# Moving a low-part subtraction from GpSimd to VectorE, and the attention output tiles out of PSUM by ScalarE

## What is computed

```python
def attend(q, k, v, lam):
    s = einsum('bhmqd,bhmkd->bhmqk', q, k) * (B_QK ** -0.5)
    p = softmax(s)
    w = p[:, :, 0] - lam * p[:, :, 1]
    return einsum('bhqk,bhkv->bhqv', w, v)

def diffattn_out(o, subln_w, lam_init):
    return (rmsnorm(o, subln_w) * (1.0 - lam_init)) ...
y_b = diffattn_out(attend(...)) * silu(bz)
```

## Time and profile before

| | |
|---|---|
| median of 3 runs | 2773.3 us (2772.2 to 2774.69) |
| profiled execution | 2774.32 us, span 2772.5 us |
| mean granted TensorE clock | 0.932 |
| PE busy | 2469.1 us (89%) |
| DVE busy | 1277.5 us (46%) |
| ACT busy | 1020.1 us (37%) |
| POOL busy | 882.3 us (32%) |
| POOL low parts, L2552, 254 instructions | 567.2 us |
| DVE low parts, L1833, 254 instructions | 377.3 us |

### The profile page before, as it was taken

The page is one execution under the profiler, slowest core; times in us unless marked ns, Lnnn a source line. Parts: engine busy times, 40 slices in busy tenths (PEclk is TensorE's granted clock), DMA queues, the critical chain, the costliest instruction groups (busy, mean ns, idle before and its releaser), DMA issues.

```text
span 2772.5 us, 39336 instructions
## 1 busy us (share of the span) xinstructions
PE 2469.1 (89%) x16496; PEld 2207.5 (80%) x16496; DVE 1277.5 (46%) x2428; ACT 1020.1 (37%) x1845; POOL 882.3 (32%) x594
## 2 busy tenths in 40 slices
PE   6999999988868999959889998987888999988998
PEld 3877768877756897848879888987767999857998
DVE  4322222555642212453333664236655674556673
ACT  2333312333331222234333444344244444344443
POOL 2222322422211233223335443442312454312453
PEclk9899999999989999978989999998899999989999
DMA  5211124211112312222214223444212455303444
GB/s 229 87 61 61 46 92 167 77 46 61 46 61 94 140 71 76 85 64 92 92 63 150 92 77 117 152 159 142 102 47 106 156 181 177 125 31 107 154 176 142
DMA packets 50416, 291.51 MB, mean 105 GB/s; under 512 B 8960, under 2 KB 13312, under 8 KB 19072
## 3 DMA queue, kind: packets, MB, share of 16 engines
q1 hardware_dynamic: 50240, 289.00, 29.4%
HBM read 286.89 MB, written 2.36 MB: 104 GB/s over the span
## 4 chain that ended last, share of the span: by engine, by line
PE 73%; DVE 14%; ACT 5%; DMA 3%; issue 2%; POOL 2%; SPq 1%; DVEq 0%; ACTq 0%; POOLq 0%
PE PS L478 71%; DMA raw<-in_wpk 2%; ACT wh L1304 2%; DVE TM L1814 2%; DVE wl L1833 2%; PE PS L482 2%; DVE colS L1822 1%; ACT TM L1294 1%; DVE HYl L1822 1%; DVE TM L1822 1%; POOL wl L2552 1%; ACT TMG L1294 1%; POOL TM L2544 1%; DVE small L1814 1%; ACT HYh L1294 1%
## 5 line engine op out<-in xcount | busy, mean ns | idle before, releaser
L2552 POOL TENSOR_TENSOR wl<-raw,wh 128x768 fp32r<-128x768 f32 (+2 forms) x254 | 567.2, 2233 | 1437.9 <-ACT wh L1305 1437.7
L478 PE MATMUL PS<-HYh,wh 128*128 128x256 f32 (+1 forms) x3000 | 966.7, 322 | 63.6 <-DVE HYl L1822 30.6
L478 PE MATMUL PS<-HYl,wh 128*128 128x256 f32 (+1 forms) x3000 | 948.8, 316 | 0.0
L478 PE MATMUL PS<-HYh,wl 128*128 128x256 f32 (+1 forms) x3000 | 946.9, 316 | 0.0
L1833 DVE TENSOR_TENSOR wl<-raw,wh 128x1280 fp32r<-128x1280 f32 (+2 forms) x254 | 377.3, 1485 | 748.7 <-ACT wh L1304 748.6
L478 PEld LDWEIGHTS PS<-HYh,wh 128*128 128x128 f32 x3000 | 589.9, 197 | 114.3 <-DVE HYl L1822 35.6
L478 PEld LDWEIGHTS PS<-HYh,wl 128*128 128x128 f32 x3000 | 588.2, 196 | 31.8
L478 PEld LDWEIGHTS PS<-HYl,wh 128*128 128x128 f32 x3000 | 589.5, 197 | 29.5
L1294 ACT ACTIVATE TM<-PS 128x512 f32<-128x512 f32 (+5 forms) x315 | 163.3, 530 | 772.6 <-PE PS L478 600.7
L1304 ACT ACTIVATE wh<-raw 128x1280 fp32r<-128x1280 f32 (+2 forms) x254 | 306.4, 1206 | 374.3 <-PE PS L478 219.1
L478 PE MATMUL PS<-wh,HYh 128*128 128x256 f32 x1458 | 429.3, 294 | 10.1 <-DVE HYl L1822 5.4
(11 more groups left out here) (174 smaller groups left out, 2041.6 us busy)
## 6 DMA issues: line engine op xcount, KB each, us to landing
raw<-in_wpk SPq DMA_DIRECT2D x235, 1024.0 KB, 4.8
raw<-in_wpk SPq DMA_DIRECT2D x32, 704.0 KB, 4.1
TM<-in_wpk SPq DMA_DIRECT2D x4, 1024.0 KB, 18.2
X<-in_xin SPq DMA_DIRECT2D x1, 2048.0 KB, 10.0
Y<-in_wpk SPq DMA_DIRECT2D x2, 1024.0 KB, 23.9
Y<-bias_d SPq DMA_DIRECT2D x4, 512.0 KB, 9.7
raw<-in_wpk SPq DMA_DIRECT2D x3, 512.0 KB, 3.8
T<-in_tabs SPq DMA_DIRECT2D x1, 1216.0 KB, 14.7
```

Source lines behind the costliest of these rows:

```text
L478: return P.x.matmul(o, l, r, start=start, stop=stop)
L2552: G.x.tensor_tensor(wl[:, s, c:n], raw[:, r, c:n], wh[:, s, c:n], ALU.subtract).then_inc(*lo_rest.mark(u))
```

## The change

It has two parts.

The low part of columns c:n is made by DVE too, as a second instruction right behind the first; POOL's `convert` and all its calls are taken out, with the signal `lo_rest`. PE and SP wait for `lo_split` alone.

In branch B, ACT writes the squares of a tile into `b_yt` and then copies bank 5's part over them, and the event `b_osq` stands for this copy. There are two `b_yt` now, used by turns, and two sets of four sums. PE's wait for `b_yo` before a new group is gone; ACT waits instead, at the first tile of a group, until PE has turned the `b_yt` of two groups before. DVE's root and four products, now from and to `b_yt` in SBUF, stand at `b_done_slot`, in layer 0 one slot later than before; the output step of layer 0 stands eight and four slots behind the last value product, where it was three.

```diff
@@ b_yt, slots
-        b_yt = tm(9728, [4, 128])
-        b_p, b_junk = TMG[:, 0:1024].rearrange("p (m k) -> p m k", m=2), TMG[:, 1024:1152]
+        b_yt = [x.rearrange("p (i c) -> p i c", i=4) for x in (tm(9728, [512]), TMG[:, 1024:1536])]
+        b_p = TMG[:, 0:1024].rearrange("p (m k) -> p m k", m=2)
+        def b_done_slot(l, p, g):
+            if l == 0 and p == 3:
+                return (71, 73)[g]
+            return b_value_slot(l, p, 4 * g + 3) + (2, 1)[l]
         def b_out_slot(l, p, g):
             if p == 3:
                 return (72, 74)[g] if l == 0 else 58
-            return b_value_slot(l, p, 4 * g + 3) + (3, 3)[l]
+            return b_value_slot(l, p, 4 * g + 3) + ((8, 4), (3,))[l][g]
@@ TensorE
             def weights(u):
                 P.wait_ge(lo_split, u)
-                P.wait_ge(lo_rest, u)
...
                     if before := b_prev(l, *pj):
                         P.wait_ge(act_step, ("b_osq", l, *before))
-                        if pj[1] % 4 == 0:
-                            P.wait_ge(dve_step, ("b_yo", l, before[0], before[1] // 4))
@@ ScalarE
                     A.wait_ge(pe_step, ("b_pv", l, *pj))
-                    if i == 0 and (before := b_prev(l, *pj)):
-                        A.wait_ge(dve_step, ("b_yo", l, before[0], before[1] // 4))
+                    k = b_group(l, pj[0], pj[1] // 4)
+                    if i == 0 and k >= 2:
+                        A.wait_ge(pe_step, ("b_yt", l, *((pj[0] - 1, pj[1] // 4) if l == 0 else (pj[0] - 2, 0))))
+                    y = b_yt[k % 2][:, i]
+                    act(y, bank(5)[:, 128 * i:128 * i + 128], ACT.Square, scale=128.0 ** -0.5, accum_out=colC[:, 44 + 4 * (k % 2) + i:45 + 4 * (k % 2) + i])
                     A.wait_own(act_step)
-                    act(b_junk, bank(5)[:, 128 * i:128 * i + 128], ACT.Square, ("b_osq", l, *pj), scale=128.0 ** -0.5,
-                        accum_out=colC[:, 32 + i:33 + i])
+                    act(y, bank(5)[:, 128 * i:128 * i + 128], ACT.Copy, ("b_osq", l, *pj))
@@ VectorE, convert
-                c, s, r = cut_of(u), slot(u), u % NRAW
+                n, c, s, r = words[u], cut_of(u), slot(u), u % NRAW
                 D.wait_ge(hi_split, (u, 0))
-                D.x.tensor_tensor(wl[:, s, 0:c], raw[:, r, 0:c], wh[:, s, 0:c], ALU.subtract).then_inc(*lo_split.mark(u))
+                D.x.tensor_tensor(wl[:, s, 0:c], raw[:, r, 0:c], wh[:, s, 0:c], ALU.subtract).then_inc(*lo_split.mark())
+                D.wait_ge(hi_split, (u, 1))
+                D.x.tensor_tensor(wl[:, s, c:n], raw[:, r, c:n], wh[:, s, c:n], ALU.subtract).then_inc(*lo_split.mark(u))
@@ VectorE, slot_b
-                if (pj := B_VALUES[l].get(n - 1)) and pj[1] % 4 == 3:
-                    p, g = pj[0], pj[1] // 4
-                    k = b_group(l, p, g)
-                    D.wait_ge(act_step, ("b_osq", l, *pj))
-                    root(small[:, 40:44], small[:, 44:48], colC[:, 32:36], more=colC[:, 36 + 4 * (k % 2):40 + 4 * (k % 2)])
+                if pg := B_DONE[l].get(n):
+                    p, g = pg
+                    k = b_group(l, p, g) % 2
+                    D.wait_ge(act_step, ("b_osq", l, p, 4 * g + 3))
+                    root(small[:, 40:44], small[:, 44:48], colC[:, 44 + 4 * k:48 + 4 * k], more=colC[:, 36 + 4 * k:40 + 4 * k])
                     D.wait_own(dve_step)
-                    if k:
-                        D.wait_ge(pe_step, ("b_yt", l, p - (g == 0), 0 if l or g else 1))
                     for i in range(4):
                         a, t_, nk = b_tile(l, 4 * g + i)
-                        stt(b_yt[:, i], bank(5)[:, 128 * i:128 * i + 128], small[:, 40 + i:41 + i], b_z[p % 2][:, t_, a], ALU.mult, ALU.mult,
-                            ("b_yo", l, p, g))
+                        stt(b_yt[k][:, i], b_yt[k][:, i], small[:, 40 + i:41 + i], b_z[p % 2][:, t_, a], ALU.mult, ALU.mult, ("b_yo", l, p, g))
@@ GpSimd: gone, with all its calls
-            def convert(u):
-                if u is None:
-                    return
-                n, c, s, r = words[u], cut_of(u), slot(u), u % NRAW
-                G.wait_ge(hi_split, (u, 1))
-                G.x.tensor_tensor(wl[:, s, c:n], raw[:, r, c:n], wh[:, s, c:n], ALU.subtract).then_inc(*lo_rest.mark(u))
@@ SyncE, load
                     if units[b][1] == "conv":
                         S.wait_ge(lo_split, b)
-                        S.wait_ge(lo_rest, b)
```

More of the change, by code:

```diff
@@ L245, in program @@
         dve_step = signal("dve_step")
-        lo_rest = signal("lo_rest")
         pool_step = signal("pool_step")
@@ L415, in program @@
                                        for f in (b_score_slot, b_turn_slot, b_value_slot))
-        B_OUT = [{b_out_slot(l, p, g): (p, g) for p in range(4) for g in range(2 - l)} for l in range(2)]
+        B_DONE, B_OUT = ([{f(l, p, g): (p, g) for p in range(4) for g in range(2 - l)} for l in range(2)] for f in (b_done_slot, b_out_slot))
         B_QK = ({13: 0, 15: 1}, {10: 0, 11: 1})
@@ L774, in slot_b @@
                     for i in range(4):
-                        t = turned(bank(6)[:, 128 * i:128 * i + 128], b_yt[:, i])
+                        t = turned(bank(6)[:, 128 * i:128 * i + 128], b_yt[b_group(l, *pg) % 2][:, i])
                     t.then_inc(*pe_step.mark(("b_yt", l, *pg)))
@@ L2544, in tt @@
                 return G.x.tensor_tensor(o, a, b, op).then_inc(*pool_step.mark(*events))
-            def convert(u):
-                if u is None:
-                    return
-                n, c, s, r = words[u], cut_of(u), slot(u), u % NRAW
-                G.wait_ge(hi_split, (u, 1))
-                G.x.tensor_tensor(wl[:, s, c:n], raw[:, r, c:n], wh[:, s, c:n], ALU.subtract).then_inc(*lo_rest.mark(u))
-            def used(tag, j):
-                convert(unit_after(place[tag, j]))
             def branch_a(l):
                 t0, N = lay(l)
-                used("gate", l)
                 G.wait_ge(dve_step, ("a_rc", l))
@@ L2570, in branch_a @@
                         tt(a_g[:, c, 0:N], a_g[:, c, 0:N], a_hs[:, c, 0:N], ALU.mult, ("a_gate", l, h))
-                    used("a_z", 4 * l + h)
                     for j in range(4):
@@ L2601, in merge @@
                             total(7)
-                    used("m_" + br, 8 * l + j)
             def merge_b(l):
                 t0, N = lay(l)
-                for j in range(4):
-                    used("m_b", 8 * l + j)
                 for j in range(8):
@@ L2610, in merge_b @@
                     tt(Y[:, j, t0:512], Y[:, j, t0:512], B_GATES[j][:, 0:N], ALU.add, ("m_sum", l, "b", j))
-                    if j % 2:
-                        used("m_b", 8 * l + 4 + j // 2)
             def branch_b(l):
@@ L2700, in second_block @@
                         rope(f"ab_q{2 + j}", tm(3584 + 512 * j, [2, 256]), 2, rope1d, 128)
[L2701 to L2705, removed]
-                else:
-                    for tag, j in (("cq", 0), ("ckv", 0), ("d_q", 0), ("d_q", 1), ("d_k", 0), ("d_k", 1), ("d_v", 0), ("d_v", 1)):
-                        used(tag, j)
+                else:
                     for i in range(3):
                         rope(f"qc{i}", QC[:, 2 * i:2 * i + 2], 2, ropec, 96)
-                    used("uq", 0)
                     rope("qc3", QC[:, 6:8], 2, ropec, 96)
-                    used("ukv", 0)
                     G.wait_ge(dve_step, "kr_rope")
-                    G.wait_own(lo_rest)
                     G.wait_own(pool_step)
@@ L2719, in second_block @@
                     G.wait_own(pool_step)
-                    for j in range(4):
-                        used("cd_out", j)
-                for j in range(2):
-                    used("x_q", 2 * l + j)
-                for j in range(2):
-                    used("x_o", 2 * l + j)
                 def mid(j):
@@ L2731, in second_block @@
                 for j in range(22):
-                    used("gu", 22 * l + j)
                     if j:
@@ L2735, in second_block @@
                 mid(21)
-                for j in range(8):
-                    for i in range(2):
-                        used("dn", 16 * l + 2 * j + i)
             for o, v in ((o1024, 1 / 1024), (o128, 1 / 128), (o256, 1 / 256), (one, 1.0)):
@@ L2742, in pool_program @@
             G.x.memset(sc[:], 0.0).then_inc(*pool_step.mark("sc_zero"))
-            convert(converted[0])
             for l in range(2):
@@ L2747, in pool_program @@
                     tt(H[1][:, k], xs[:, k], H[0][:, k], ALU.subtract, ("H", l, k))
-                    if l == 0 and k == 3:
-                        convert(converted[1])
                 if l == 0:
@@ L2758, in pool_program @@
                 merge(l, "c")
-                for j in range(4):
-                    used("w_out", 4 * l + j)
             for l in range(2):
@@ L2820, in program @@
         programs = (tensor_program, scalar_program, vector_program, pool_program, sync_program)
```

(2 more changed lines are left out.)

16 lines of the change are left out of this document (removed).

## The result

| | before | changed |
|---|---|---|
| median | 2773.31 us | 2704.42 us (2695.15 to 2704.77, 4 runs) |
| ratio | | 0.9743, 95% interval 0.9722 to 0.9765 |
| profiled span | 2772.5 us | 2702.7 us |
| mean granted clock | 0.932 | 0.941 |

What follows compares the result with a forecast made beforehand. PE, busy 89%, was taken as the bound, with its waits mainly for DVE's results, held up partly by POOL. Terms -46.6 - 1.8 - 16.5 + 12.0 = -52.9 us gave 2720.5 us, range 2700 to 2752.

Steps and rivals of the forecast that it cites:

- the lock: DVE instructions with two SBUF inputs and POOL instructions reading SBUF exclude each other; one pair showed 1.85 against 0.42 us.
- the 8.2 us: Layer 0, three PE stalls at a new group's first value product, waiting for `b_yo` while POOL's work slows DVE's root.
- Part 1: Output tiles: removing waits for `b_yo` was to gain 46.6 us in layer 0 and 1.8 us in layer 1.
- the five long stalls: Layer 0 waits on `b_yo`: three of 8.2 us, and two beside the merge of 7.58 and 7.06 us.
- The new wait: Layer 0, after each 8.2 us stall: PE would wait 1.6 us for the next tile's softmax shares.
- Part 2: Low parts moved from POOL to DVE: 16.5 us gained from locks, 12 us lost at steps that only pay.
- my places: Among 122 PE gaps, 29 locked places gaining 16.5 us after paying 0.86 each, and 12 steps that only pay.
- rival 3: The locks are worth more than found on PE's path: another 25 us goes, 2696 us; chance 0.11.
- The wait that is handed on: Layer 0: the next tile's softmax replaces `b_yo`, root still locked by POOL's rotary step; 2749 us, chance 0.18.
- Slower: DVE's second low part falls ahead of steps PE waits for; with 110 of 254, 2803 us; chance 0.08.
- The wait at 167.99: PE's wait of 2.75 us for two products behind a DVE low part, to grow to 3.6 us.
- the signs: Profile after: no group-start wait over 3 us between 555 and 830, POOL near 315 us, DVE about 1390, clock above 0.932.

Runs made afterwards that it cites:

- low parts alone: Against the kernel before, only the second low part moved from POOL to DVE, branch B as before: 2748.45 us, ratio 0.9907.
- Output tiles alone: Against the kernel before, only ACT's copy of output tiles and the later slots, POOL still making its low parts: 2715.41 us, ratio 0.9787.
- the run with the early root: Changed kernel with DVE's root and products of layer 0 one slot earlier, output step at its late slots: 2712.96 us, ratio 0.979.
- the two runs that change its length: Changed kernel with DVE's second low part made twice: 2804.31 us; with it cut to 128 of 768 columns from the fifth unit on: 2651.9 us.
- the run with both engines: Output tiles as changed, POOL making its low parts as before, DVE also running a second subtraction of the same width: 2868.45 us, ratio 1.0349.
- the old slots: Changed kernel with layer 0's root, products and output step at their former slots: 2719.67 us; with only root and products one slot earlier: 2712.96 us.

## Why the prediction came out as it did

**What bounds the kernel, the lock and the reason of the 8.2 us: right.** PE is held up by the root through bank 5, and the root in part by POOL: 3.5 of its 5.9 us are lock. The rest of the 8.2 us is DVE's order, a low part and a reduce ahead of the root, and low parts alone left 7.39 us. Output tiles alone, 2715 us, is what this reading gave for part 1 (-46.6 - 1.8 = 48 us) and more.

**Part 1, size: 46.6 forecast in layer 0, 57.3 measured alone, and 59.6 with part 2.** The term that was too small is the clock. I had 8.5 us behind the five long stalls, from windows of 2.7 to 8 us behind each, and 38.1 us of standing still. With the output tiles alone PE's busy time in the stretch fell by 253.59 - 236.86 = 16.7 us and its standing still by 40.6; the mean clock of the whole stretch went from 0.88 to 0.97. So 8.2 of the 10.7 us missed are clock, twice what I had counted. The new wait that I put at 1.6 us for each of the three long stalls is about 0.75 in the changed kernel: I had the softmax of the next tile late, and overlooked what the new `b_done_slot` does. It puts the root behind the shares. That step was passed over as "one slot later", and the 10 to 13.5 us of the run with the early root hang on it. On the other side, the forecast put no charge on bank 6 beyond a few tenths; the changed kernel waits there twice, 1.8 us each.

**Part 2, forecast net -4.5 us (-16.5 and +12), measured -11 to -14 as the difference to the output tiles alone** (in stages +14 and -29). The sum came out near, its terms did not. The second piece costs 0.33 to 0.40 us on the path for each of its microseconds, by the two runs that change its length. 248 us of it are then 82 to 99 us, where my places gave 12 + 25 = 37. As the sum is -11 to -14, POOL's low parts must have cost some 95 to 110 us, where I had 41 (16.5 and the 25 paid at those places). This last number is an estimate from a slope on both sides of the changed kernel, not measured by a run of its own; the run with both engines could only bound it. It is also not all shown to be lock. DVE's other instructions became 203 us shorter, which by the slope of 0.33 to 0.40 is 67 to 81 us; the rest may be locked steps that stood nearer to PE's than the average, or POOL's own queue and later weights, and no run separates these. What was mis-sized is the count, on both sides: I looked at the instruction right ahead of each of 122 gaps. My explanation, which no run follows step by step, is that DVE's delay is carried through several of its instructions, and through ACT, to a gap that shows nothing locked in front of it. The group by form said it more plainly, and I had it in rival 3:

```profile
L1818 DVE TENSOR_TENSOR TM<-TM 128x256 f32<-128x256 f32 x96 | 40.5, 424 | 4.5
```

424 ns, for 1268 in the earlier trace rows, 81 us in this form alone. I expected 0.9, for I believed POOL's rotary steps held it up too; all 96 start after 1821 us, in the second block, and are at their undisturbed 0.42 once the low parts have left POOL.

**The rivals.** The wait that is handed on (2749 us) did not come, but two runs brought it about by the old slots, at 4.0 and 3.9 us three times each: it was kept off by the later root, not by chance. "The locks are worth more" (2696) was right in that the locks were worth more than I had found, but what the second piece costs was larger too and took most of it back. The rule of the Trainium skill cited there (page "Perfetto Trace Analysis", section "Optimizing Scalar/DVE Operations"), by which a move between these two engines may not help, holds here to this extent: of an estimated 100 us that POOL's low parts had cost, some 90 went into DVE's own queue; low parts alone still gained 25.5 us. "Slower" was nearer than I thought. With another 250 us on DVE the kernel is 30 us slower than before.

**The losses named.** The wait at 167.99 grew from 2.75 to 3.62 us, by 0.87 as forecast, and branch A of layer 0 and layer 1 lost time as I said. PE's waits for `wl` fell from 3.6 + 3.0 to 5.1 us, though the longest rose from 3.6 to 5.1. Of the signs: no first product of a group waits any more; POOL is busy 335.9 us (about 315 forecast: its own steps became longer beside DVE's low parts, `TM<-TM,wtab` from 1021 to 1206 ns); DVE 1322.9 (1390 forecast; its other instructions gave back 203 us and not 100).

## What to carry to other kernels

Where PE waits for a PSUM bank, ask who has to read it and what stands before that reader; a copy by an engine with room frees the bank, but here the gain was whole only when the work that had been waited for was put behind the steps that PE needs next. An engine at 49% is not free: with in-order queues and PE at its heels, each microsecond put on DVE here cost 0.33 to 0.40. When two engines become one, set the split between pieces anew; it was worth 16 us here, about as much as the move of the low parts brought on top of the output tiles (11 to 14).

## What the runs showed of the hardware

A DVE instruction with two SBUF operands that starts beside a POOL low part is not merely slowed. In the run with both engines it stood until POOL's had ended and then did its own work: 2170.56 to 2172.98 beside POOL's 2169.74 to 2172.16, where it needs about 0.9 us by itself; in the mean 2196 ns of 217 instructions, for 1003 without POOL's low part. Even steps on 128x4 words take 0.5 to 1.1 us beside POOL instead of 0.16, and a TENSOR_SCALAR of 128x4 words 0.66 instead of 0.17. I had expected that of wide instructions and not that thirteen tiny ones would take 5.9 us instead of 2.4. It works both ways: POOL's `TM<-TM,wtab 128x256` went from 1021 to 1206 ns in the mean when DVE took over the low parts.
